# A two-layer streaming encoder trunk on one core: layers written out, first loads reordered, clears and fetches moved

## The reference, cut to what matters

```python
x = x + 0.5 * rms_norm((silu(g) * u) @ w_down, norms[1])   # FFN 1: g, u = split(rms_norm(x, norms[0]) @ w_gu)
h = rms_norm(x, norm_mix[0]); P = h @ w_in                 # one projection; attention, recurrence, convolution on P
x = x + rms_norm(concat(A, B, C) @ w_out, norm_mix[1])
x = half_ffn(x, norm_ffn2, ...)                            # FFN 2, as FFN 1
```

## Time and profile before

| what | value |
|---|---|
| median of 3 runs (lowest to highest) | 3256.18 us (3256.08 to 3257.55) |
| profiled execution, first to last instruction (span) | 3254.3 us |
| median less span (the profiled execution's time is shown by its span alone) | 1.9 us |
| mean granted TensorE clock | 0.937 |
| busy: PE / PEld / DVE / ACT / POOL | 88% / 82% / 47% / 29% / 15% |
| DMA moved | 209.5 MB, 64 GB/s over the span |

### The profile page before, as it was taken

One profiled execution on the slowest core, in us unless ns is written; L12 is line 12 of the kernel. 1 busy time (PEld: TensorE's weight loads), 2 busy tenths in 40 slices (PEclk: granted clock), 3 DMA queues, 4 the chain that ended last, 5 costly groups with the idle time before them and its releaser, 6 DMA issues. The chain is left out here.

```text
span 3254.3 us, 44093 instructions
## 1 busy us (share of the span) xinstructions
PE 2851.5 (88%) x18054; PEld 2665.5 (82%) x18054; DVE 1528.1 (47%) x1886; ACT 944.0 (29%) x1237; POOL 476.2 (15%) x328
## 2 busy tenths in 40 slices
PE   1999998997477979999969999989955788999997
PEld 1899998894354879999969999979834458999997
DVE  1633333528965353333353333352499644433333
ACT  1322223216423332212232212231362342322221
POOL 1100001105812120000120000020084313000001
PEclk9999999998768989999989999999976798999998
DMA  5122212113010212122112122122120111212211
GB/s 108 65 71 71 78 63 79 65 52 98 1 73 7 72 52 78 59 83 73 57 60 84 62 81 77 57 73 78 36 76 15 59 46 46 78 68 75 78 61 63
DMA packets 50676, 209.51 MB, mean 64 GB/s; under 512 B 13928, under 2 KB 14312, under 8 KB 34568
## 3 DMA queue, kind: packets, MB, share of 16 engines
q1 hardware_dynamic: 50568, 208.05, 19.3%
HBM read 197.85 MB, written 10.19 MB: 64 GB/s over the span
## 5 line engine op out<-in xcount | busy, mean ns | idle before, releaser
L291 PE MATMUL ps<-hr,wr 128*128 128x320 f32 x11424 | 1707.5, 311 | 83.6 <-DVE hr L407 65.7
L291 PEld LDWEIGHTS ps<-hr,wr 128*128 128x128 f32 x11424 | 1692.3, 189 | 99.7 <-DVE hr L407 43.5
L291 PE MATMUL ps<-hid,wr 128*128 128x320 f32 x4224 | 620.8, 309 | 0.0
L291 PEld LDWEIGHTS ps<-hid,wr 128*128 128x128 f32 x4224 | 619.8, 188 | 0.0
L286 DVE TENSOR_TENSOR wr<-stage,wr 128x2048 fp32r<-128x2048 f32 x184 | 421.7, 2292 | 299.7 <-ACT wr L282 299.7
L282 ACT ACTIVATE wr<-stage 128x2048 fp32r<-128x2048 f32 x184 | 350.6, 1905 | 557.5 <-PE ps L291 288.9
L548 DVE TENSOR_TENSOR arena<-ps,arena 128x640 f32<-128x640 f32 x88 | 72.5, 824 | 545.5 <-PE ps L291 543.8
L523 POOL TENSOR_TENSOR arena<-arena 128x640 f32<-128x640 f32 x28 | 44.3, 1582 | 1737.0 <-ACT arena L499 1737.0
L490 ACT ACTIVATE arena<-arena 128x640 f32<-128x640 f32 x88 | 65.1, 739 | 801.8 <-DVE arena L548 801.8
L860 POOL TENSOR_TENSOR proj<-proj,arena 128x640 f32<-128x640 f32 x120 | 200.1, 1669 | 33.6 <-ACT arena L1018 16.9
L938 PE MATMUL ps<-proj 128*128 128x256 f32 x264 | 90.9, 519 | 97.5 <-issue 78.4
(11 more groups left out here) (204 smaller groups left out, 2224.5 us busy)
## 6 DMA issues: line engine op xcount, KB each, us to landing
stage<-in_wgu SPq DMA_DIRECT2D x88, 1024.0 KB, 4.8
stage<-in_wd SPq DMA_DIRECT2D x32, 768.0 KB, 4.2
stage<-in_w_in SPq DMA_DIRECT2D x24, 1024.0 KB, 4.8
stage<-in_wd SPq DMA_DIRECT2D x32, 640.0 KB, 3.8
stage<-in_w_out SPq DMA_DIRECT2D x8, 1024.0 KB, 5.0
arena<-in_ic SPq DMA_DIRECT2D x16, 256.0 KB, 2.8
hf<-bias_table SPq DMA_DIRECT2D x2, 2048.0 KB, 10.7
arena<-in_kc SPq DMA_DIRECT2D x16, 256.0 KB, 5.2
```

The costliest lines, as they stand in the source:

```text
L291: mm = pe.matmul(out, w(s), v(t), start=start and n == 0, stop=stop and n == 2)
```

## The change

The layer loop becomes a Python loop, so that both layers' instructions are written out one after the other. `sem` returns the same semaphore for the same name, and both FFNs of a layer share the tag "ffn". The first FFN's Lead is `opening`: it leaves out the scaling of y and the addition to x. SP's first loads come in a new order: par, one eighth of x, slot 0, the rest of x in two parts, slot 1, then the constants. The table's scratch moves from `proj` to `y`; its write to DRAM moves from SP in the opening block to ACT's queue in the first FFN block, behind the norm, and DVE's wait for it to the first down product. The next layer's `par` and slots 0 and 1 are loaded at the end of FFN 2 (`then_next`). `w_in` and `par_in` are no longer cleared; their waits count on. POOL clears the `ffn_` semaphores in the projection block and those of the mixer in FFN 2; the block between layers clears 24.

```diff
-        scratch = proj[:].rearrange("p c n -> p (c n)")
+        scratch = y.rearrange("p k n -> p (k n)")
...
+                sp.dma_start(par[:], ins["params"][0]).then_inc(par_in, 16)
+                sp.dma_start(x[:, 0], ins["x"][:, 0]).then_inc(x_in[0], 16)
+                load(sp, 0, 0, first_slot(0, 0))
+                sp.dma_start(x[:, 1:4], ins["x"][:, 1:4]).then_inc(x_in[1], 16)
+                sp.dma_start(x[:, 4:KD], ins["x"][:, 4:KD]).then_inc(x_in[2], 16)
+                load(sp, 0, 1, first_slot(0, 1))
                 for dst, src in ((cst[:], ins["consts"]), (t_rel, ins["rel_bias"]),
                                  (t_hot, ins["bucket_hot"]), (t_lbe[:, 0:4], ins["lb"])):
                     sp.dma_start(dst, src).then_inc(const_in, 16)
-                sp.dma_start(x[:], ins["x"]).then_inc(x_in, 16)
-                sp.wait_ge(table_ready, 2)
-                sp.dma_start(ins["table"], t_neg.unsqueeze(1).to_broadcast([8, 128, NREL])).then_inc(table_out, 16)
...
-                pool.memset(y, 0.0).then_inc(ones_ready, 1)
...
-                self.act_root_y(act)
+                if not self.opening:
+                    self.act_root_y(act)
                 for k in range(KD):
-                    act.wait_ge(self.x_ready, k + 1)
+                    if self.opening:
+                        act.wait_ge(x_in[X_CHUNK[k]], 16)
+                    else:
+                        act.wait_ge(self.x_ready, k + 1)
...
                     lead.act_norm(act)
+                    if lead.opening:
+                        act.wait_ge(table_ready, 2)
+                        act.dma_start(ins["table"], t_neg.unsqueeze(1).to_broadcast([8, 128, NREL])).then_inc(
+                            table_out, 16)
...
+                    if n0 == FFN2:
+                        for s in early_sems():
+                            pool.sem_clear(s)
...
-        with nc.Fori(0, DEPTH) as l:
-            def open_layer(sp, gate_up):
-                sp.dma_start(par[:], ins["params"][l]).then_inc(par_in, 16)
-                for j in range(2):
-                    load(sp, FFN1, j, gate_up(0, j))
+        for l in range(DEPTH):
+            before["slots"] = NSLOT * l
...
+            def then_next(sp):
+                sp.dma_start(par[:], ins["params"][l + 1]).then_inc(par_in, 16)
+                if l < DEPTH - 1:
+                    for j in range(2):
+                        sp.wait_ge(w_lo, NSLOT + j - 1)
+                        load(sp, 0, j, first_slot(l + 1, j))
...
-            clear(all_sems)
+            clear([w_hi, w_lo, used, evac] + ffn_sems())
```

More of the change, by code:

```diff
@@ L255, in _ @@
                         pool.sem_clear(s)
-        w_in = [sem(f"w_in{j}") for j in range(2)]
+        w_in = [sem(f"w_in{j}", True) for j in range(2)]
         w_hi, w_lo = sem("w_hi"), sem("w_lo")
@@ L266, in build @@
         FFN2 = OUTP + 4
+        NSLOT = FFN2 + KF + 2 * KD
+        before = {"slots": 0}
         def load(sp, n, j, src, size=WSLOT):
@@ L279, in split_hi @@
         def split_hi(act, i, j, n0):
-            act.wait_ge(w_in[j], i * 16 + (8 * n0 + 16))
+            act.wait_ge(w_in[j], i * 16 + (8 * (n0 + before["slots"]) + 16))
             act.activation(wr[:, j, 0], stage[:, j], ACT.Copy).then_inc(w_hi, 1)
@@ L318, in ones_sum, with first_slot, _ @@
             mm.then_inc(done, 1)
+        def first_slot(l, j):
+            return ins["wgu1"][l, j]
+        with nc.Block() as block:
+            @block.sync
+            def _(sp):
+                sp.dma_start(par[:], ins["params"][0]).then_inc(par_in, 16)
[4 more added lines that the diff above has]
+                load(sp, 0, 1, first_slot(0, 1))
+                for dst, src in ((cst[:], ins["consts"]), (t_rel, ins["rel_bias"]),
+                                 (t_hot, ins["bucket_hot"]), (t_lbe[:, 0:4], ins["lb"])):
+                    sp.dma_start(dst, src).then_inc(const_in, 16)
+            @block.tensor
+            def _(pe):
+                pe.wait_ge(const_in, 64)
+                for c in range(2):
+                    pe.matmul(ps[0:8, c, 0:NREL // 2], t_rel, t_hot[:, c * (NREL // 2):(c + 1) * (NREL // 2)],
+                              start=True, stop=True).then_inc(table_mm, 1)
+            @block.scalar
+            def _(act):
+                for c in range(2):
+                    act.wait_ge(table_mm, c + 1)
+                    act.activation(t_neg[:, c * (NREL // 2):(c + 1) * (NREL // 2)], ps[0:8, c, 0:NREL // 2],
+                                   ACT.Copy, scale=8.0).then_inc(table_ready, 1)
+                act.wait_ge(lb_step, 3)
+                act.activation(t_lbe[:, 0:4], t_lbe[:, 4:8], ACT.Exp).then_inc(lb_exp, 1)
+            @block.gpsimd
+            def _(pool):
+                pool.memset(ones[:], 1.0).then_inc(ones_ready, 1)
+            @block.vector
+            def _(dve):
+                dve.wait_ge(const_in, 64)
+                l0, l1 = t_lbe[:, 0:2], t_lbe[:, 2:4]
+                dve.tensor_tensor(t_lbm[:, 0:2], l0, l1, ALU.max).then_inc(lb_step, 1)
+                dve.wait_ge(lb_step, 1)
+                dve.tensor_tensor(t_lbe[:, 4:6], l0, t_lbm[:, 0:2], ALU.subtract).then_inc(lb_step, 1)
+                dve.tensor_tensor(t_lbe[:, 6:8], l1, t_lbm[:, 0:2], ALU.subtract).then_inc(lb_step, 1)
+                dve.wait_ge(lb_exp, 1)
+                dve.tensor_tensor(t_lbm[:, 0:2], l0, l1, ALU.add).then_inc(lb_step, 1)
+                dve.wait_ge(lb_step, 4)
+                dve.reciprocal(t_lbm[:, 2:4], t_lbm[:, 0:2]).then_inc(lb_step, 1)
+                dve.wait_ge(lb_step, 5)
+                dve.tensor_tensor(t_lbe[:, 4:6], l0, t_lbm[:, 2:4], ALU.mult).then_inc(lb_step, 1)
+                dve.tensor_tensor(t_lbe[:, 6:8], l1, t_lbm[:, 2:4], ALU.mult).then_inc(lb_step, 1)
+                dve.wait_ge(lb_step, 7)
+                dve.tensor_tensor(t_lb[:, 2:4], t_lbe[:, 4:6], t_lbe[:, 6:8], ALU.add).then_inc(lb_step, 1)
+                dve.tensor_tensor(lb_all[:, 0, 0:2], t_lbe[:, 4:6], t_lbe[:, 4:6], ALU.subtract).then_inc(lb_step, 1)
+                dve.wait_ge(lb_step, 8)
+                dve.tensor_tensor(lb_all[:, 1, 0:2], t_lb[:, 2:4], t_lbe[:, 4:6], ALU.subtract).then_inc(lb_step, 1)
+                dve.wait_ge(lb_step, 10)
+                dve.tensor_scalar(lb_all[:, :, 2:4], lb_all[:, :, 0:2], -1.0, 1.0, ALU.mult, ALU.add).then_inc(lb_step, 1)
@@ L320, in build, with __init__ @@
         class Lead:
-            def __init__(self, tag, n0, factor, post, pre):
-                self.n0, self.factor, self.post, self.pre = n0, factor, post, pre
+            def __init__(self, tag, n0, factor, post, pre, opening=False):
+                self.n0, self.factor, self.post, self.pre, self.opening = n0, factor, post, pre, opening
                 self.y_factor = sem(f"{tag}_y_factor")
@@ L374, in pool_part @@
             def pool_part(self, pool):
-                pool.wait_ge(self.y_total, 1)
+                if not self.opening:
+                    pool.wait_ge(self.y_total, 1)
                 pool.memset(ssum, 0.0).then_inc(self.summed, 1)
@@ L396, in dve_part @@
             def dve_part(self, dve):
-                self.dve_start(dve)
-                self.dve_y(dve, 0)
+                if not self.opening:
+                    self.dve_start(dve)
+                    self.dve_y(dve, 0)
                 for s in range(KD + 1):
-                    if s < KD:
+                    if s < KD and not self.opening:
                         self.dve_x(dve, s)
-                    if s < KD - 1:
+                    if s < KD - 1 and not self.opening:
                         self.dve_y(dve, s + 1)
@@ L416, in dve_norm, with early_sems, ffn_sems @@
                 dve.wait_ge(self.rsqrt, 1)
+        def early_sems():
+            running = (w_hi, w_lo, used, evac)
+            return [named[n] for n in named
+                    if named[n] in all_sems and named[n] not in running and not n.startswith("ffn_")]
+        def ffn_sems():
+            return [named[n] for n in named if n.startswith("ffn_")]
         def ffn(l, tag, n0, wgu, wd, lead, first, after, ahead):
@@ L569, in _ @@
                         last = bool(f0)
+                        if lead.opening and not last:
+                            dve.wait_ge(table_out, 16)
                         with dve.Fori(0, KD // 2 - last) as i:
@@ L611, in _ @@
                     lead.pool_part(pool)
+                    for s in ffn_sems():
+                        pool.sem_clear(s)
                 @block.vector
@@ L1575, in _ @@
             def _(dve):
[L1576 removed]
+                dve.wait_ge(par_in, 16 * (DEPTH + 1))
                 last.dve_start(dve)
```

91 lines of the change are left out of this document (20 added, 71 removed).

## The result

The changed kernel takes 3185.49 us (median of 4 runs, 3184.31 to 3186.98); the kernel before, on the same chip, 3256.86 (3256.08 to 3260.11). The ratio is 0.978 (95% interval 0.9767 to 0.9792, further on in square brackets): 71.4 us less. The forecast was 3180.0 in 3173 to 3198. The profiled execution took 3186.98 us, with a span of 3184.9; its fall against the profiled span of before (3254.3) is 69.4.

A forecast was written before the change was run, and what follows sets the result against it. Nearly everything but the mixers was taken to run at TensorE's rate; gains of 60.1 + 11.7 + 4.6 = 76.4 us from span 3254.3 gave 3177.9, plus 1.9 for the median: 3180, range 3173 to 3198 (8 in 10).

The forecast's parts named there:

- Opening: Kernel's start up to slot 1: early par, x and slots and no work on zero y gain 60.1 us.
- What arrived at 4.16 arrives at 16.1: Opening: constants, now behind 4.78 MB of loads at 401 GB/s (11.9 us), land at 16.1 instead of 4.16.
- DVE's first low part of x takes 0.9: Opening's FFN block: DVE's step after slot 0's split takes 0.9 us, so the first product starts at 25.7.
- behind the wait: Opening's Lead: without the warm-up root, the root's functions are fetched behind the wait, a table load costing 1.3 us.
- The table on ACT's queue: First FFN block: moving the table's write costs 0, since slot loads beside it have about 20 us of room.
- even a tripled load of 1 MB fits in the room: Slot loads beside the table's write: 2.6 us at 401 GB/s plus latency, tripled, still fits about 20 us.
- The prediction's own sign of being wrong: First FFN block: an idle row of ACT at line 282 behind a slot's load between 60 and 110 us.
- Boundary: Between the layers: fewer clears, no loop branch and early loads bring the reciprocal 11.7 us earlier, ends 8 to 12.1.
- end: Kernel's end: fewer clears and sums at full clock gain 4.6 us, between 2.7 and 5.0.
- slower: Rival, chance 0.03: written-out code makes turns of TensorE's loops stall 3.9 us each for code, 3336 us.
- sum: Whole kernel: 60.1 + 11.7 + 4.6 = 76.4 us off the profiled span of 3254.3, giving 3177.9.
- the front moves but stays late: Rival, chance 0.12: opening's constants behind 4.8 MB at 288 GB/s, Lead paced by POOL; 5 to 8 us lost, 3185 to 3188.

The follow-up runs named there:

- run 8: Changed kernel, kernel before and run 1's kernel repeated unaltered for second profiles: 3183.73 us, and 3255.27 and 3172.21 us in one execution each.
- run 7: Changed kernel with POOL's eight additions of squares left out of the opening's FFN block (output differs): 3180.49 us in one execution.
- run 2: Changed kernel with the bias table's write back on SP's queue, behind the first loads, instead of ACT's: 3206.14 us.
- Run 6: Kernel before without TensorE's and POOL's wait for par at the start of a layer: 3253.01 us in one execution, kernel before beside it 3256.31.
- run 4: Changed kernel with layer 2's par and slots 0 and 1 loaded only at that layer's start, the last par in the last block: 3189.68 us.
- run 5: Changed kernel with the mixer's semaphores cleared in the block between layers again, instead of by POOL inside FFN 2: 3191.0 us.
- run 1: Changed kernel with the four small loads of constants moved from the end of SP's first loads to right behind par: 3173.92 us.

## Why the prediction was right, and where it was off

- **Opening, 60.1 predicted, 59.8 measured.** The mechanism holds. "What arrived at 4.16 arrives at 16.1": 16.04 (16.22 and 16.80 in the executions of runs 8 and 7), so 401 GB/s was about the right rate. "The FFN block starts at 20.6": 20.59. Two terms were wrong and cancelled. "DVE's first low part of x takes 0.9" took 2.1, since POOL's sums run beside it (run 7), and the first product came at 27.04, not 25.7: 1.3 late. The table load of 1.3 "behind the wait" ran ahead of it, at 39.34, hidden: 1.3 less. Slot 0 took 16.70 where 16.3 was charged. That 59.8 stands so near to 60.1 is luck in this part.
- **The table on ACT's queue, 0.** Right in the total, but at its edge. ACT was not held: its issue took 1.29 us, and DVE's half of slot 2's split came 9.8 us behind slot 1's start (55.38), as in the kernel before (115.20). But loads of 4.7 us without the write became 9.4 to 20.6, and the room of 20 us was all used (a wait of 1.01). The Trainium skill, "DMA: Bandwidth & Descriptors", section "Queues, rings and completion order", says that the two queues share 16 engines and alternate by packets. Loads that are slowed but not blocked (14.7 median) agree with the sharing. That the turns are as short as one packet of the profile is not borne out: from 62 to 68 us only the write moved, at 50 GB/s, while slot 4's load was out. On one queue the load was blocked (run 2, a wait of 22.62). The step "even a tripled load of 1 MB fits in the room" was too small: the slowest took 4.4 times as long (20.6 against 4.7). The prediction's own sign of being wrong, an idle row of ACT behind a slot's load between 60 and 110, did appear, with 1.01 us.
- **Boundary, 11.7 predicted, 12.2 measured; end, 4.6 and 4.3.** The sums began at the full rate (0.35 us a pair), as the forecast took it, though the last pairs took 0.56. The path was the one named, the split by ACT and DVE: the reciprocal follows 4.15 us behind the split's start. Run 6 bears out the reading of the branch, which lay beside the path; runs 4 and 5 bear out the loads and the clears. The rival "slower", turns of TensorE's loops that stall for code, did not come: layer 1's FFN 2, from its reciprocal to DVE's last addition, takes 484.87 us written out and 484.85 in the loop.
- **The step that was off: "sum"**, which held everything else unchanged. The three terms make 76.3 of 76.4, the profiled pair 69.4 and the medians 71.4. The rest of the program is not the same from execution to execution: 7.1 us in two stretches of one program. The forecast's own range, 3174 to 3185, had room for 5 us upward for its terms, and none for this, and the measured 3185.49 lies just outside it. By its number it would fit the rival "the front moves but stays late" (3185 to 3188); the rows rule that out, since slot 1 started at 45.62 where 45.3 was forecast. The stated range, 3173 to 3198, held the time because it was made wide enough for rivals as well. A part of some 3 us may belong to the written-out form; that is open.

## What to carry to other kernels

Ask of the first loads what each holds up: first loads behind a slow write on one queue cost 31 us here, and constants behind 4.8 MB another 11. A second queue keeps a slow transfer from blocking loads, but not from slowing them, so count the room of the loads beside it. When the sum of the local gains and the total differ by a few us, profile the same program twice before looking for a cause in the diff.

## What the runs showed that was not expected

A write of 2.69 MB from 8 partitions takes some 56 us on either queue (7.0 to 63.4 before, 44.9 to 102 after), and slows a 1 MB load from 4.7 to as much as 20.6 us, though the packets of the two queues fill only 35.2 + 22.5% of the 16 engines' time from 44 to 106 us. The trace's packets show how the load of slot 4 went: 64 of its 128 packets had begun by 61.9, and none of the slots' began from then to 68.7. In these 6 us the write moved its 50 GB/s and took 0.46 of the engines' time, so the other half waited while half of that time was free. A likely reason is that the write works through half of the engines only, and that this half of the load had to pass through the same ones; the trace does not name the engine of a packet, so that is not shown.

The length of the attention stretch goes with TensorE's granted clock, which differs between executions of one program. Windows of attention alone in layer 1, run 1's kernel, first and second execution:

```profile
873.97:1007.10 133.13, 111.00 (x614) 68.54 (x613) 75.63 (x171) 54.53 (x142) 33.13 (x34) 0.89 0.14 49
```

```profile
878.18:1014.97 136.79, 115.36 (x614) 70.87 (x613) 75.69 (x172) 54.55 (x142) 33.13 (x34) 0.85 0.13 48
```

As an estimate from these rounded means, 0.89 between the two levels 1.00 (2.4 GHz) and 0.50 (1.2 GHz) is 29 us at the low level, and 0.85 is 41: 12 us more there, and the stretch 3.7 longer, 0.3 us for each. The engines other than TensorE were busy equally long. What makes the clock fall at another moment the second time, with the same code and the same data, no run here shows.
